# The order of one vector engine's work in an attention step: where the first fill evacuations of a step stand against the next step's row maximum

## The reference, cut to what matters

```python
s = jnp.einsum('bqhd,bkhd->bhqk', qi, k).astype(jnp.float32) * scale
s = jnp.where(mask, s, NEG)
p = jax.nn.softmax(s, axis=-1)
...
branches = jnp.stack([y_a * silu(a_z), y_b * silu(b_z), y_c * silu(c_z)], axis=2)
proj_br = jnp.einsum('blnw,nwd->blnd', branches, w_branch)
merged = jnp.sum(sigmoid(gates) * proj_br, axis=2)
return x + merged @ w_out
```

## Time and profile before

| what | value |
|---|---|
| median of 3 runs | 4000.63 us (3999.26 to 4002.53) |
| the profiled execution | 3993.1 us, of it 3990.6 us span |
| TensorE busy | 3853.0 us, 97% |
| VectorE busy | 2120.4 us, 53% |
| ScalarE busy | 927.2 us, 23% |
| GpSimd busy | 1190.4 us, 30% |
| steps of layer 0 of the second block | about 2574 to 3182 us |
| steps of layer 1 | about 3308 to 3890 us |

### The profile page before, as it was taken

One profiled execution on the slowest core, in us unless ns is written; L12 is line 12 of the kernel. 1 busy time (PEld: TensorE's weight loads), 2 busy tenths in 40 slices (PEclk: granted clock), 3 DMA queues, 4 the chain that ended last, 5 costly groups with the idle time before them and its releaser, 6 DMA issues.

```text
span 3990.6 us, 68645 instructions
## 1 busy us (share of the span) xinstructions
PE 3853.0 (97%) x27284; PEld 3092.8 (78%) x27284; DVE 2120.4 (53%) x4770; ACT 927.2 (23%) x2306; POOL 1190.4 (30%) x962
## 2 busy tenths in 40 slices
PE   8999999999999999999999999899999999999999
PEld 3666678878886666668887888687887788888778
DVE  5666665575413666566466611533446662444566
ACT  4223321112101233222102200323232212232221
POOL 0113315434442022223443444101333231143322
PEclk9999999999999999999999999999999999999999
DMA  3011102222222210111222222211211231121222
GB/s 128 31 44 43 34 20 87 90 64 90 90 85 69 64 48 28 34 38 64 89 86 72 85 89 89 77 54 59 61 59 61 80 102 59 54 64 59 64 64 96
DMA packets 70956, 266.57 MB, mean 67 GB/s; under 512 B 7872, under 2 KB 8000, under 8 KB 69872
## 3 DMA queue, kind: packets, MB, share of 16 engines
q1 hardware_dynamic: 68160, 246.42, 19.7%
q10 hardware_dynamic: 2480, 15.76, 1.1%
HBM read 253.64 MB, written 8.52 MB: 66 GB/s over the span
## 4 chain that ended last, share of the span: by engine, by line
PE 91%; DVE 5%; issue 1%; DVEq 1%; ACT 1%; ACTq 0%; DMA 0%; PEld 0%; PEldq 0%; SPq 0%
PE ps L2651 32%; PE ps L1582 15%; PE ps L1608 10%; PE ps L2607 10%; PE ps L1627 2%; PE ps L1709 2%; PE ps L955 2%; PE ps L1769 2%; PE ps L911 2%; PE ps L2618 1%; PE ps L1728 1%; PE ps L2665 1%; PE ps L2679 1%; PE ps L945 1%; PE ps L1097 1%
## 5 line engine op out<-in xcount | busy, mean ns | idle before, releaser
L2651 PE MATMUL ps<-arena,ring 128*128 128x256 f32 x1856 | 430.3, 379 | 0.0
L2607 PE MATMUL ps<-xT,ring 128*128 128x512 f32 x864 | 385.4, 601 | 7.2 <-ACT xT L2815 6.3
L2651 PEld LDWEIGHTS ps<-arena,ring 128*128 128x128 f32 x1856 | 352.6, 190 | 47.9
L2651 PE MATMUL ps<-arena 128*128 128x256 f32 x1536 | 360.9, 379 | 0.0
L2524 POOL TENSOR_TENSOR arena<-ring 128x512 f32<-128x512 f32 (+1 forms) x120 | 145.8, 1215 | 695.9 <-DMA ring<-in_weights 582.5
L2382 POOL TENSOR_TENSOR arena<-ring 128x512 f32<-128x512 f32 x50 | 63.9, 1279 | 969.0 <-DMA ring<-in_weights 732.0
L2607 PEld LDWEIGHTS ps<-xT,ring 128*128 128x128 f32 x864 | 162.9, 192 | 210.9 <-issue 209.8
L2651 PEld LDWEIGHTS ps<-arena 128*128 128x128 f32 x1536 | 291.8, 190 | 39.7
L2651 PE MATMUL ps<-xT,ring 128*128 128x256 f32 x896 | 207.5, 385 | 13.9 <-ACT xT L2815 11.8
L1608 PE MATMUL ps<-arena,ring 128*128 128x264 f32 (+1 forms) x896 | 205.2, 385 | 4.2 <-DVE arena L2123 1.7
L2651 PEld LDWEIGHTS ps<-xT,ring 128*128 128x128 f32 x896 | 172.8, 193 | 40.4 <-issue 16.2
(11 more groups left out here) (425 smaller groups left out, 7422.5 us busy)
## 6 DMA issues: line engine op xcount, KB each, us to landing
ring<-in_weights SPq DMA_DIRECT2D x459, 512.0 KB, 3.5
h_dram<-arena ACTq DMA_DIRECT2D x2, 2112.0 KB, 6.8
arena<-h_dram ACTq DMA_DIRECT2D x2, 2112.0 KB, 9.2
arena<-skew_dram ACTq DMA_DIRECT2D x8, 448.0 KB, 3.2
arena<-in_x SPq DMA_DIRECT2D x1, 2048.0 KB, 8.1
out_rows<-arena SPq DMA_DIRECT2D x8, 256.0 KB, 2.9
skew_dram<-arena ACTq DMA_DIRECT2D x4, 511.5 KB, 6.8
consts<-in_const SPq DMA_DIRECT2D x1, 1256.0 KB, 10.6
```

What stands on the lines that cost most here:

```text
L2607: m = pe.matmul(o, w[:, k, :], src[:, k, 0:S], start=k == 0, stop=k == KD - 1)
L2651: m = pe.matmul(bank_of(i, n), w[name][:, k, :], x[name](k), start=start and k == ks[0], stop=stop and k == ks[-1], skip_group_check=True)
```

## The change

On VectorE alone, inside the loop over the steps, the evacuations of `fill(n, "a")` now come ahead of `rowmax(n + 1)`. Where step n+1 has "ms" units, the old order stays. No instruction is added or removed, and no other engine's list is touched. Of the 108 steps 92 take the new order, and in 76 of these VectorE has work in `fill(n, "a")` together with a row maximum to pass it.

```diff
                     probs_scaled(n)
                     if n > mine[0]:
                         gated(n - 1)
+                    late = (n + 1, "s") not in POINTS
+                    if late:
+                        fill(n, "a")
                     if n < mine[-1]:
                         rowmax(n + 1)
-                    fill(n, "a")
+                    if not late:
+                        fill(n, "a")
                     fill(n, "b")
```

## The result

The changed kernel takes 4006.02 us (median of 20 runs, 3998.78 to 4011.24) where the kernel before takes 3999.93 us on the same chip (20 runs, 3994.81 to 4004.20). The ratio is 1.0015, 95% interval 1.0008 to 1.0022: 6 us more (3 to 9), inside the 0.2% that was set as the bound of "no change", but not zero. The profiled execution took 4002.41 us, its span 4000.6 us.

What follows compares the result with a forecast made beforehand. TensorE, busy 3853.0 of 3990.6 us, was taken as the bound. Terms -6.1 + 2.3 + 1.8 + 1.6 - 0.5 + 1.0 = +0.1 us, applied to the median 4000.63, gave 4000.7 us, range 3996 to 4007.

Steps and rivals of the forecast that it cites:

- the cancelling sum: Whole kernel: gains and losses nearly cancel at +0.1 us, 4000.7 us; own range 3998 to 4004; chance 0.65.
- the branch-C chain: Rival: row maximum ends last in branch C's 34 steps; each losing 0.5 us gives 4011.5 us; chance 0.12.
- six waits: Steps 42, 47, 52, 94, 98, 102: TensorE's waits for a fill bank behind a row maximum go, -6.1 us.
- step 65: Row maximum of step 66 goes ahead of L2095, TensorE waits at L1627: +2.3 us, bounds 0 and +2.4.
- steps 37, 89: Ends of branch B: scaling and next row maximum come later, +0.9 us each, +1.8 together; bounds 0 and +3.2.
- steps 93, 97: Many VectorE units in fill b: 0.8 us later each, +1.6; nothing taken for held operations; bounds 0 and +7.2.
- late branch C: Turn at 3165.72: its probs_scaled can start up to 0.5 us earlier, -0.5 us; bounds -1.0 and +1.4.
- late row maxima, three places: Steps 53, 58, 106: row maximum starts later than the turn's slack allows, +1.0 us in sum; bounds 0 and +3.
- "only the gain" rival: Whole kernel: the six waits go and the priced losses find cover, 3994 us; chance 0.15.
- no twin near 3013: The wait L1665 on L2259 was to grow, with a twin wait near 3013.
- The signs: Profile after: L1728 waits on L2297 exceed 1.8 us; at 10 us in all the branch-C chain holds.
- "L2114 gone": Profile after: the waits L1608 and L1582 on L2123, L2156 and L2114 were to be gone.

Runs made afterwards that it cites:

- experiment 1: Kernel before, with the new order only in steps 42, 47, 52, 94, 98 and 102: 3992.84 us, ratio 0.9987 to the kernel before.
- experiment 12: New order only in steps 42, 47, 52, 94, 98 and 102, measured again on another chip: 3993.66 us, ratio 0.9977 to the kernel before.
- experiment 2: The change, with steps 65, 93 and 97 in the old order: 3998.56 us, ratio 0.9998 to the kernel before.
- experiment 4: The change, with GpSimd's four weight sums left out for each of two pairs beside steps 93 and 97: 4002.71 us, a single execution.
- experiment 6: Kernel before, with the new order only in branch C without 42, 47, 52, 94, 98, 102, 93, 97: 4009.15 us, ratio 1.0028.
- experiment 8: The change, with the row maximum in 65, 93 and 97 also behind the first one or two units of fill b: 4001.04 us, ratio 1.0008.
- experiment 9: The change, with steps 65, 93, 97, 41, 46, 51, 58, 101 and 104 in the old order: 3994.14 us, ratio 0.9980.
- experiment 11: Kernel before, with the new order only in steps 42, 47, 52, 94, 98, 102, 41, 46 and 101: 3999.49 us, ratio 0.9993.
- experiment 5: Kernel before, with the new order only in branches A and B without step 65: 3997.84 us, ratio 1.0000.
- experiment 10: Kernel before, with the new order only in steps 51, 58 and 104: 4009.92 us, ratio 1.0021.
- experiment 3: Kernel before, with the new order only in steps 65, 93 and 97: 4007.64 us, ratio 1.0016.

## Why the prediction came out as it did

It said 4000.7 us and the median is 4006.02, inside its range of 3996 to 4007. The mechanism, gains in six places against losses in a few others, holds; the sizes of the single terms do not all. That the median falls inside is in part luck: it lies outside the 3998 to 4004 of the cancelling sum itself, by 2 us, and within what the range had added for the branch-C chain, which is not what happened. In us, by the increases of the table above:

| term of the sum | said | measured |
|---|---|---|
| six waits | -6.1 | -4.1 (alone: -7.0) |
| step 65 | +2.3 | +2.2 |
| steps 37, 89 | +1.8 | 0 |
| steps 93, 97 | +1.6 | +4.3, and 1.6 by the clock |
| late branch C | -0.5 | 0 |
| late row maxima, three places | +1.0 | +2.3 at three, two of them others |
| sum | +0.1 | +4.7, and 1.6 + 1.45 by the clock |

From turn 0 to turn 107 the whole increase is 8.35 us; the 0.6 us that the table lacks are small increases of about 0.1 us each. The two profiled executions are 9.3 us apart, the medians 6.1.

- **The six waits.** Each is what was said, as experiments 1 and 12 show. In the profile of the change only four are collected (-0.88 and three times -1.32, together -4.84). Turns 42, 43 and 47 lose 0.70 instead. In that trace the scaling of step 42 is one of 1.51 us, behind an L2291 held for 1.19 us, and it, not the row maximum, now stands ahead of L2114 at 3050.18, since row maximum 42 was late and held (L2277, 1.07 us) in step 41. This belongs to the execution and not to the order alone. Experiments 2 and 4 have the same order in layer 0, and turns 43 and 48 gain 0.84 and 0.91 us there. In experiment 2 the same L2291 isn't held, and L2114 is done 0.6 us ahead of the turn:

```profile
3051.09 0.16 DVE L2291 TENSOR_TENSOR arena<-arena 128x2 f32<-128x2 f32 x1 [0.16 <-ACT arena L1961]
...
3053.03 0.42 DVE L2114 TENSOR_TENSOR arena<-ps,consts 128x264 f32<-128x264 f32 x1
...
3054.08 0.60 PE L1728 MATMUL ps<-consts,arena 128*128 128x128 f32 x4
```

The six turns have -6.4 us in experiment 2 and -6.6 in experiment 4, so the term was sized nearly rightly. What the prediction missed are the neighbours' own turns: it looked at each of the six as if its neighbour kept the old order. Turn 52 is on time in the profile of the change and comes 1.08 to 1.26 us late in experiments 2, 4, 6 and 8; experiments 9 and 11 show that the neighbours cost something, and the traces that how much falls to each varies (turn 42: 0.15 after, 1.27 in experiment 11).

- **Step 65.** Right in place, line and size: 2.13 us at L1627 behind L2095. Nothing covered it, which was the point against the "only the gain" rival. Experiment 8 shows that it can't be had by going further back either.
- **Steps 37 and 89.** The wait at L1665 is 0.70 us beside 0.63, and no twin near 3013 exists. The lower bound held, and experiment 5 measures the whole of A and B at nothing. What absorbed the later row maximum wasn't looked at in an experiment.
- **Steps 93 and 97: the step that failed.** This is the term that was mis-sized most. The prediction put them at 2.3 - 0.33 - 1.17 = 0.8 us each, and took "none" of the holding by GpSimd, "since other held operations leave the same stretch in exchange". Two things were wrong. The loss was sought at the turn, yet it came 6.7 us ahead of it (3775.64, the turn standing at 3782.34), at the bank that L2114 frees: the larger idle spell, 1.17 us, stands *behind* L2114 and could not serve it. And the exchange gave back only the 0.39 us of turn 94. L2125 and L2136 are still long after the change (1.24 and 1.76 us). Unheld the bank wait is 0.62 us, held 2.59 (experiment 4), and the turns come 0.30 and 0.29 us late instead of 2.27 and 3.61: the row maximum itself costs less than the 0.8 us said, and the holding, put at nothing, is with the clock behind it nearly the whole term. The upper bound of +7.2 stood in the text and covers the 4.3. A reading behind it was wrong too: in step 102 of the kernel before, what GpSimd ran beside L2275 and L2279 were not its weight sums but the rotations. They end at 3855.11 and 3856.52, the two held operations at 3855.14 and 3856.54:

```profile
3853.84 1.27 POOL L2414 TENSOR_TENSOR arena<-arena,consts 128x512 f32<-128x512 f32 x1 [0.18 <-issue]
...
3855.26 1.26 POOL L2416 TENSOR_TENSOR arena<-arena 128x512 f32<-128x512 f32 x1
```

So the rotations hold small operations as the sums do.

- **Late branch C.** The turn of the earlier trace rows waits 0.50 us instead of 0.52. Its scaling now waits for the exponentials (L2291 is released by L1961 at 3165.53), which start later because the row maximum does. The two shifts cancel.
- **Late row maxima.** Step 58 does what was said (turn 59 waits 0.36 us, said 0.4). But I sought such steps only among 53, 58 and 106, by the distance between turns. The costly ones are 51, 101 and 104, where VectorE has two or three evacuations of a pair in `fill a`, for whose products it waits. At step 51 the row maximum starts at 3125.88 where it started at 3120.37: 4.0 us later, beyond the 1.5 us by which the turn itself has shifted. In the profile of the change turn 52 just bears that; in experiment 8 it comes 1.26 us late.
- **The branch-C rival** (every step loses x = 0.41 us or more) is refuted in its form: experiment 9 keeps the new order in all but eight steps of branch C, and turns lose nothing. Its size was closer than its chance of 0.12 says, though: the rest of branch C costs 11 us when it isn't met by the six (experiment 6). In the change the two largest increases (+3.67 at turn 43, +4.85 at turn 53) are absent, because there the six steps are late as well: with the next row maximum behind `fill a`, it no longer adds to the late scaling ahead of the bank, as it does in experiment 10. Experiment 11 shows it for turn 43: 41 late and 42 late too gives -0.84, 41 late and 42 old gives +3.67 (experiment 6).
- **The signs.** L1728 on L2297 grew from 1.8 to 2.5 us, far from the 10 of the chain case. "L2114 gone" failed: its wait at the old places went, and new ones of 4.9 us came at steps 93 and 97.

TensorE's clock adds what no order of instructions explains. Windows of the profile after (columns: stretch, length, busy time and count of PE, PEld, DVE, ACT and POOL, granted clock, DMA share, GB/s):

```profile
3310.00:3330.00 20.00, 20.00 (x80) 16.45 (x80) 6.66 (x23) 3.15 (x13) 0.00 (x0) 0.84 0.25 79
3420.00:3430.00 10.00, 9.50 (x86) 8.71 (x87) 8.12 (x13) 3.45 (x6) 0.00 (x0) 1.00 0.14 52
3776.00:3790.00 14.00, 14.00 (x80) 11.28 (x79) 10.59 (x29) 2.98 (x11) 2.91 (x3) 1.00 0.13 38
3818.00:3828.00 10.00, 10.00 (x48) 7.73 (x47) 7.88 (x18) 1.33 (x5) 2.72 (x3) 0.83 0.04 8
```

Behind the wait of 2.35 us at step 97 the granted clock is 0.83 in the mean, part of the stretch being at 1.2 instead of 2.4 GHz, and eight matmuls take 3.07 us, where the same eight take 1.99 behind the 2.59 us wait of step 93 with the clock at 1.00. Together with the L1769 group (1.12 instead of 0.66) that is some 1.6 us for step 97. Near 3310, where no instruction was moved, the clock is 0.84 and was 0.94 before. That this differs from one execution to the next is shown by experiments 1 and 12: the same kernel has an increase of -1.63 us at turn 60 in one and of 0.01 in the other, and over all experiments it lies between -1.64 and +3.22. So the price of such a wait varies too. With 4.7 us in waits, about 1.5 of the median's 6 us are left for that; this split is argued, not measured.

What stays open: why 51, 58 and 104 alone cost 8 us by the medians, where their trace has 6.4 at the three turns, and why the six gain 5 us in one comparison and 9 in the other, where both traces have about 7. The clock behind long waits may carry the first; the intervals, 3.6 us on either side, allow for all of it.

## What to carry to other kernels

When an item in an engine's list is moved back, follow the *next* consumer in the list, not the item's own: the losses here stood at the bank freed by the unit behind the row maximum, and one step on, where a late scaling and a row maximum stood together. Price a move against the neighbours in their new order as well. A global reordering can be split: six of the steps carry the whole gain (0.9987 and 0.9977), and with nine steps back in the old order the loss of the change is gone (0.9980); a condition that names the steps is worth more than the rule.

A small VectorE operation on SBUF that lands beside GpSimd's large sums or rotations should be priced to the end of the running one (0.16 us becomes 1.1) wherever somebody waits behind it. Which of several is held can vary from one execution to the next.

## What the runs showed of the hardware

- Held small operations end with GpSimd's. In the same step, with GpSimd at its sums or idle, L2275 takes 1.17 or 0.17 us and L2279 1.12 or 0.16. The Trainium skill (SBUF - State Buffer, section "Who interferes with whom") says that whoever issues first keeps the shared ports for its whole instruction. The trace agrees: L2275 and L2279 end 0.02 and 0.01 us behind the sums beside them, while L2277 between them takes 0.16 us. Priced at the 2.0 us a place that experiment 4 measured, the holding would have given the better sum.
- Waits of 2 to 4 us were followed by a lower clock in some cases (experiments 3 and 4 after 2.13 us at step 65, both with 0.83 over 3420 to 3430; experiment 10 after 4.26, the change after 2.35) and not in others (the change after 2.13 and after 2.59 us). Experiment 10's window, stretch as above:

```profile
3142.50:3149.50 7.00, 6.78 (x29) 4.98 (x30) 3.61 (x10) 2.25 (x8) 2.60 (x2) 0.76 0.27 76
```

- Some short waits don't show in the rows of TensorE's matmuls, whose ends the profile models, but in those of its weight loads. The waits of weight loads for L2297 between 2560 and 3910 are 6.2 us in 9 waits after and 3.4 in 4 before, where the matmuls' rows have 2.5 and 1.8.
